# A hybrid encoder layer on one core: another order of the last tile's attention units

## The reference

```
h = LN(x) * (1 + scale) + shift ;  q, k, v of two head groups = h @ w_in
A) 8 heads of neighbourhood attention on an 8 x 64 token grid, learned relative bias
B) 4 heads of differential attention, T5 relative bias:
   w = softmax(q1 k1 + bias) - lambda * softmax(q2 k2 + bias);  o = w @ v
   o = o * rsqrt(mean(o*o) + eps) * subln * (1 - lambda_init)      # per head of 128 columns
x = LN(alpha*x + (1+gate) * concat(A, B) @ w_out)
u = LN(x) * (1 + scale) + shift
PEER: query = u @ w_query; top 16 x top 16 product keys -> 16 experts for each of 8 heads
      out = sum over 8*16 experts of gate * gelu(expert_down[e] . u) * expert_up[e]
x = LN(alpha*x + (1+gate) * out)
```

## Time and profile before

| | us |
|---|---|
| median of 3 runs (1845.85 to 1849.44) | 1847.87 |
| the profiled execution's own time | 1854.31 |
| its span in the profile | 1852.5 |
| busy: PE, DVE, POOL, ACT | 1478.9, 1122.1, 990.6, 429.0 |

### The profile page before, as it was taken

One profiled execution on the slowest core, in us unless ns is written; L12 is line 12 of the kernel. 1 busy time (PEld: TensorE's weight loads), 2 busy tenths in 40 slices (PEclk: granted clock), 3 DMA queues, 4 the chain that ended last, 5 costly groups with the idle time before them and its releaser, 6 DMA issues.

```text
span 1852.5 us, 14452 instructions
## 1 busy us (share of the span) xinstructions
PE 1478.9 (80%) x4096; PEld 696.5 (38%) x4096; DVE 1122.1 (61%) x2749; ACT 429.0 (23%) x1080; POOL 990.6 (53%) x1053
## 2 busy tenths in 40 slices
PE   5999998797898889766887986877596877777776
PEld 5444456543543344222333333432243322222222
DVE  5532166868575666656766666665564774576553
ACT  3111244423222222212222221221221221122121
POOL 2000000366666566666666666666666666666664
PEclk9999998999999999999999998999898989889899
DMA  9947301599999999999999999999999999999996
GB/s 318 356 158 189 136 24 24 196 357 360 355 363 381 390 364 358 351 375 375 366 368 391 389 373 365 361 380 378 352 358 369 380 349 383 369 347 377 368 374 259
DMA packets 188821, 606.01 MB, mean 327 GB/s; under 512 B 30895, under 2 KB 31303, under 8 KB 188583
## 3 DMA queue, kind: packets, MB, share of 16 engines
q0 software_dynamic: 147456, 536.94, 76.4%
q1 hardware_dynamic: 39943, 64.29, 10.3%
q10 hardware_dynamic: 1344, 3.87, 0.7%
HBM read 601.68 MB, written 3.34 MB: 327 GB/s over the span
## 4 chain that ended last, share of the span: by engine, by line
PE 27%; DVE 22%; issue 15%; POOL 14%; DMA 10%; another core or an unknown queue 9%; ACT 2%; SPq 0%; POOLq 0%; DVEq 0%; ACTq 0%
PE pair L862 11%; POOL big L639 10%; PE pair L649 10%; DVE big L1419 7%; DMA big<-in_expert_down,expert_idx 4%; POOL region_v L639 4%; DMA big<-in_expert_up,expert_idx 4%; DVE region_v L1419 3%; PE pair L707 2%; PE pair L681 2%; DMA region_v<-in_expert_down,expert_idx 1%; DMA big<-in_w_ada 1%; ACT big L968 1%; DVE big L1326 1%
## 5 line engine op out<-in xcount | busy, mean ns | idle before, releaser
L862 PE MATMUL pair<-big 128*128 128x512 f32 x1460 | 731.2, 629 | 215.9 <-issue 96.0
L1419 DVE CUSTOM_DVE_ANT_0 big<-big,pair 128x1024 f32<-128x1024 f32 x363 | 438.8, 1219 | 185.2 <-DMA big<-in_expert_down,expert_idx 113.8
L862 PEld LDWEIGHTS pair<-big 128*128 128x128 f32 x1460 | 269.3, 197 | 595.3 <-issue 544.9
L639 POOL DMA_INDIRECT big<-in_expert_up,expert_idx x365 | 346.5, 949 | 225.7 <-issue 100.3
L639 POOL DMA_INDIRECT big<-in_expert_down,expert_idx x363 | 344.9, 950 | 131.2 <-issue 99.9
L862 PE MATMUL pair<-region_v,big 128*128 128x512 f32 x588 | 290.4, 618 | 75.3 <-DMA region_v<-in_expert_up,expert_idx 38.3
L1051 ACT ACTIVATE big<-ident,big 128x128 f32<-128x128 f32 x512 | 167.1, 391 | 310.4 <-issue 148.5
L1419 DVE CUSTOM_DVE_ANT_0 region_v<-region_v,pair 128x1024 f32<-128x1024 f32 x149 | 181.3, 1219 | 81.3 <-DMA region_v<-in_expert_down,expert_idx 57.2
L639 POOL DMA_INDIRECT region_v<-in_expert_up,expert_idx x147 | 139.9, 951 | 108.2 <-remote 41.1
L862 PEld LDWEIGHTS pair<-region_v,big 128*128 128x128 f32 x588 | 106.2, 195 | 217.9 <-issue 197.9
L639 POOL DMA_INDIRECT region_v<-in_expert_down,expert_idx x149 | 143.0, 960 | 54.5 <-issue 40.9
(11 more groups left out here) (150 smaller groups left out, 1050.0 us busy)
## 6 DMA issues: line engine op xcount, KB each, us to landing
big<-in_w_ada SPq DMA_DIRECT2D x8, 2048.0 KB, 21.7
big<-in_w_in SPq DMA_DIRECT2D x6, 2048.0 KB, 13.2
big<-in_w_query SPq DMA_DIRECT2D x5, 2048.0 KB
big<-in_w_ada SPq DMA_DIRECT2D x16, 512.0 KB, 17.7
big<-in_expert_up,expert_idx POOLq DMA_INDIRECT x365
big<-in_expert_down,expert_idx POOLq DMA_INDIRECT x363
big<-in_w_out SPq DMA_DIRECT2D x2, 2048.0 KB
big<-na_scr SPq DMA_DIRECT2D x24, 128.0 KB, 4.4
```

Of the source, the lines that this page charges most:

```text
L639: nc.gpsimd.indirect_dma_start(places[place], None, (expert_down if kind == "down" else expert_up)[0], bass.IndirectOffsetOnAxis(expert_id ...
L862: last = nc.tensor.matmul(pair[t % 2][:, s * HALF:(s + 1) * HALF], diag[:, j, :], places[place][:, s * HALF:(s + 1) * HALF], start=(h == 0 ...
L1419: v.tensor_tensor_reduce(out=places[place], in0=places[place], in1=u_cur[:, :], scale=1.0, scalar=0.0, op0=ALU.mult, op1=ALU.add, accum_ou ...
```

## The change

The last tile's units run in another order, and what is derived from the order follows: the last neighbourhood unit is now the last of all (unit 31), and the last differential one is unit 29. The gather that reuses the T5 bias waits for the scores of unit 29 instead of the last unit. Where two differential units follow each other (24 after 23, 29 after 28), VectorE waits for the earlier one's exponentials before it writes `diff_raw`. The sums of squares and the scaling of the tile before are tied to the place in the tile, eighth and first, instead of to a unit's number; they stay in the slots in which they were.

```
-LAST_UNIT = UNITS[-1]
-ATT = [(t, u) for t in range(TILES) for u in UNITS]
+LAST_UNITS = [4, 0, 5, 1, 6, 7, 2, 3]
+ATT = [(t, u) for t in range(TILES) for u in (UNITS if t < TILES - 1 else LAST_UNITS)]
 LAST_NA = max(a for a, (_, u) in enumerate(ATT) if u < NA_PAIRS)
+LAST_DIFF = max(a for a, (_, u) in enumerate(ATT) if u >= NA_PAIRS)
...
                 elif n == 1:
-                    pool.wait_ge(dve_evac, EVAC[INDEX[("scores", (last, 1))]][1])
+                    pool.wait_ge(dve_evac, EVAC[INDEX[("scores", (LAST_DIFF, 1))]][1])
...
                         scored, dst = ps[:, :], diff_raw[:, m, :]
+                        if a > 0 and not is_near(a - 1):
+                            dve.wait_ge(exp_done, 2 * a)
...
-                    if u == LAST_UNIT:
+                    if a % len(UNITS) == len(UNITS) - 1:
...
-                    if u == UNITS[0] and t > 0:
+                    if a % len(UNITS) == 0 and t > 0:
```

## The result

Over 20 runs of each, the changed kernel takes 1853.44 us (1847.68 to 1858.9), the kernel before 1847.53 us (1843.81 to 1855.59). The ratio is 1.0034, interval [1.0024, 1.0043]: 6 us slower, where 0.4 us was forecast, outside the range. The profiled execution took 1851.39 us with a span of 1849.6 us, less than the 1852.5 of before: one execution of each scatters by more than the change is worth, so the two spans say nothing. What follows goes by ratios over many runs and by the stretch around 350 us.

What follows compares the result with a forecast made beforehand. The DMA stream of expert gathers was taken to bound the kernel. Dot 8's shift of -0.5 to +1.2 us, taken as +0.4, made the span 1852.9 us and the time 1848.3 us, range 1844.6 to 1851.8.

Steps and rivals of the forecast that it cites:

- What bounds the kernel: Whole kernel: the DMA stream of expert gathers; each microsecond of DMA idleness after its start costs one at the end.
- Part 1: Last tile's attention: gathers 1 and 2 issued 5.6 us earlier, near 344.2 us, and both in by 349.5.
- Part 2's working: Second query chunk's load, released by unit 31's scores: issued near 350.0 us, 4.5 us later than before.
- at 0.4 MB per us the weights (2.10 MB) are in at 357.2: SP queue after the attention: the query weights' flow starts at 351.9 us and ends at 357.2.
- TensorE's 358.0: Time in us at which TensorE was expected to be ready for the second chunk's queries; weights due about 0.8 earlier.
- the even share: DMA queues: weights share with gather 3 from 354 us, landing near 360 instead of 357.2; 1848.6 us, chance 1 in 5.
- So the weights' delay is hidden: Start of the query products: late weights cost nothing, by about 0.8 us, with 1.7 us more hidden at the first Gelu.
- Part 3: Tail after unit 31: last VectorE copy near 355.2 us, 0.4 us earlier; bounds 1.0 us later and 0.8 earlier.
- Part 4: VectorE ahead of units 24 and 29: new waits on the earlier unit's exponentials, 0 us, up to 0.5.
- The sum: Start of the up products, set by dot 8: shift between -0.5 and +1.2 us, taken as +0.4.
- The late load: Slower rival: low clock makes VectorE wait in slots 28 to 31, weights at 359.7, dot 8 +3.7 us; 1851.6, chance 0.15.
- The faster rival: Early gathers keep DMA engines full from 352 us and the hole at 377 closes: -2.5 us, 1845.4, chance 0.19.

Runs made afterwards that it cites:

- the old order's late load: Kernel before, order kept, with only the second query chunk's load waiting for unit 31's scores instead of unit 30's; 1.004 of before.
- the runs with the query products behind the ups: Second chunk's query products and key scores moved behind the first up products, in the changed kernel (1.0038 of before) and in the kernel before (1.0051).
- split load: Changed kernel with the second query chunk loaded in two halves, the first into space free since slot 22; 1.0004 of before.
- the run with the late T5 wait: Changed kernel, new order kept, but gather 1 waits for unit 31's scores again instead of unit 29's; 1.0007 of before.
- its repeat: The changed kernel run and profiled again without an edit; 1.0036 of before.
- TensorE kept busy: Changed kernel with 12 needless 128x128 products on TensorE just ahead of its wait for the weights; 1.0022 of before.
- the later pause: Changed kernel in which GpSimd waits for the report of the fourth query product before gather 14; 1.0006 of before.
- the rows late: Changed kernel with the 1 MB load of the LN rows held back until the fourth query product is reported; 1.003 of before.

## Why the prediction was wrong

- *What bounds the kernel* held. The stream runs at 0.97 of the DMA engines behind 1000 us in both kernels, and the loss is a hole at its start. That a microsecond of the hole is one of the time holds roughly: 6.2 us of delay at gather 16 against gather 0 and 5.9 us of median in after; 6.9 and 7.4 us (0.4%) with the old order's late load. It is no law: the runs with the query products behind the ups have gather 16 where before has it, within 0.3 us, and lose 0.4 and 0.5% behind it.
- *Part 1* held. Gather 1 went out at 343.82 (344.2 forecast), and gathers 1 and 2 were in by 349.9.
- *Part 2's working* held up to the issue: the load goes out at 349.49 (350.0). The step that failed first is "at 0.4 MB per us the weights (2.10 MB) are in at 357.2". By 356 us SyncE's queue had moved 1.82 of the 2.10 MB; at 0.4 MB per us, with the queue to itself, the rest would have been in at 356.7 (an estimate from these two numbers). The last packet of the weights ends at 358.44 and TensorE starts at 359.00, 1 us past what I had called TensorE's 358.0, and 1.8 later relative to gather 4 than before. I had read the earlier trace rows as the SP queue shutting out the gathers. It was their delay: gather 1's first byte came 4.7 us behind its issue at 349.81, when the weights were already in. Gather 3 in after needs 4.2 us (351.68 to 355.89) and in the next two microseconds they take nearly half. From 356 to 358 us of after (packets, MB, share):

```profile
q1 hardware_dynamic: 172, 0.43, 57.6%
q0 software_dynamic: 92, 0.36, 45.8%
```

  The Trainium skill (DMA: Bandwidth & Descriptors, section Queues, rings and completion order) has each DMA engine go round the queues that have work, a packet at a time; to the even share that I drew from it I had given 1 in 5. This trace agrees with it, with 57.6 and 45.8% of the engines' time while both queues had bytes to move, and I should have seen that the earlier trace rows could not speak against it, with hardly any gather bytes ready to be moved.
- *"So the weights' delay is hidden"*, with 1.7 us more behind the Gelu, is the step that carries the loss. I priced lateness at its own length. It is paid three more times: the idle TensorE falls to its low clock (+1.6 and +0.9 us, of which keeping it busy gave back 1.6), and its reports come late (+4.9). The low clock was in my reach, as the earlier trace rows show 0.83 in that stretch and the trace of before shows 0.50 behind a microsecond in which TensorE stood still:

```profile
344.00:345.00 1.00, 0.00 (x0) 0.03 (x1) 0.93 (x8) 0.85 (x3) 0.00 (x0) 1.00 0.00 0
...
347.00:348.00 1.00, 1.00 (x4) 0.00 (x0) 0.70 (x2) 0.00 (x0) 0.00 (x0) 0.50 0.75 217
```

  The late report I had overlooked. No report of before is late ahead of 372 us (none of the 162 that can be matched to a record comes over 0.3 us behind it), but behind 372 us, in the second phase, the same trace is full of them. The copy below is of a product whose last record ends at 468.82; its report comes 3.1 us later. Of the 63 waits of GpSimd of 0.4 us or more that a report of an up product ended, 56 ended with one over 0.3 us late. In the summary of GpSimd's waits in before (us in all, times, longest) those late by 1.5 us and more stand under `remote`, with a few of another engine's reports; after has 29 and 10 such waits:

```profile
467.76 1.05 PE L681 MATMUL pair<-big 128*128 128x128 f32 x8
...
471.92 0.28 ACT L950 ACTIVATE big<-pair 128x128 f32<-128x128 f32 x1 [5.93 <-remote]
```

```profile
POOL big L639 <- remote: 75.2, 36, 4.7
...
POOL region_v L639 <- remote: 41.1, 16, 4.9
```

  So a late report is no freak of the changed kernel. The late weights moved the last query products towards the part of the kernel in which TensorE's reports are often late, at a place where the whole chain to the first up product hung on one.
- *Part 3* was right in sign and too small: the last VectorE copy is at 354.33 (355.2 forecast), and gather 4 is 1.4 us earlier against gather 0 than before, not 0.4, outside the bound of 0.8. Unit 31's scores end at 349.4 instead of the 349.9 that I had added up; against gather 0 they are 0.2 us ahead of before and not 0.4 behind it. *Part 4* held: no wait ahead of units 24 and 29 is seen on VectorE.
- *The sum* went by dot 8. It starts at 370.20, inside the forecast 369.5 to 371.2, and it did not matter: the first Gelu, at 377.31, had become what the ups wait for. The forecast named queries that start after 360 us as a sign that it is wrong; they started at 359.0 and it was wrong all the same.
- *The rivals.* "The late load" was the right place with the wrong road: VectorE was not late, and the price was not in dot 8. It had 0.15. The faster rival found no support: with the start-up of before restored (split load) the two early gathers are not seen in the time, 1.0004.

What stays open is why the report is late. Shown: it moves with GpSimd's issues (the pauses before gathers 12 and 14), it does not need the LN rows' bytes, full DMA engines without GpSimd's issues do not bring it about, and it is late for every engine that waits for it. Nor was an engine waiting for its code: in after no packet of the instruction queues moves between 358 and 379 us. But GpSimd's issuing is not enough either. In before, and in the run with the late T5 wait, GpSimd issues gathers through the query products and the reports are on time; in the run with the late T5 wait it had waited 1.58 us for a dot just before the fourth product ended. The early gathers take away such waits, which would fit, but this is only argued. Each pause was profiled once. Nor do the traces tell whether the products really end when their modelled ends say.

## What to carry to other kernels

Slack on an in-order chain is not worth its length: count what the engine behind the late transfer loses while it stands still (here a clock level, and a report that came up to 5 us late). Look through the whole trace for such things and not only at the place of the change: the late reports stood in the second phase of before. Then check the chain behind it to the point where a buffer comes free. Before an order of work is changed for the sake of one release, list every other release that hangs on "the last of its kind": here the last neighbourhood unit freed 2 MB of weights that the first phase was waiting for. A transfer that moved no bytes in some stretch may not have been shut out; look for its first byte's delay behind its issue before calling a queue favoured.

## What the runs showed of the hardware that was not expected

- TensorE's signal of a finished product reached ScalarE 4.9, 4.5, 2.4, 2.5, 2.2 and 5.0 us behind the modelled end of its last matrix product in six profiles (after, its repeat, the old order with the late load, TensorE kept busy, the later pause, the rows late), where it is 0.03 to 0.04 us in before, with the late T5 wait, with the split load and with a pause before gather 12. A 1.8 us pause of GpSimd's gather issue removed it. In the second phase such reports are common: of before's 280 reports behind 372 us that can be matched to a record, 159 come over 0.3 us behind it, and none of the 162 ahead of 372 us.
- An indirect gather's first byte came 1.7 to 1.9 us behind its issue with idle DMA engines (343.82 to 345.47 in after, 336.21 to 338.14 in before) and 4.2 to 4.7 us behind it with another queue's load under way.
